# Down projection of three of four MLP quarters as seven block products per pair of weight tiles

## The chip, the cores and the metric

One core of a Trainium2 chip runs the whole kernel in one launch. The metric is the device time in microseconds (us) from start to end of an execution. Engines: TensorE (PE in the profile, its weight loads PEld), VectorE (DVE), ScalarE (ACT), GpSimd (POOL), SyncE (SP, which issues the transfers).

## The reference, cut to what matters

One layer of a hybrid decoder: 512 prompt tokens and 8 decode tokens, 1024 channels, three token mixers on one normalised input, merged by gates, then an MLP. The change is in the MLP's second matrix product:

```python
def merge_and_mlp(h, gates, y_a, y_b, y_c, w_out, norm_mlp_g, w_up, w_down):
    mixed = gates[0] * y_a + gates[1] * y_b + gates[2] * y_c
    h = h + mixed @ w_out
    hn = rmsnorm(h, norm_mlp_g)
    return h + jnp.square(jax.nn.relu(hn @ w_up)) @ w_down      # 1024 -> 4096 -> 1024
```

## The kernel before, in words

Activations lie transposed: 128 channels on the partitions, 520 tokens (512 + 8) along the free dimension, in two halves of `HALF` = 260. Each weight matrix is streamed in units of 128 output channels by 1024 input channels (`KC` = 8 blocks of 128x128, 512 KB). Every float32 operand is split in a high part (rounded to fp32r) and a low part (the rest), and a product is three matmuls of 260 columns: high x high, high x low, low x high. A tick is one unit with one half: 8 blocks x 3 = 24 matmuls into one PSUM bank. `TICKS` lists them in TensorE's order (`project`); VectorE's `take` reads the bank after each tick.

A unit goes through these hands: SyncE loads it (`load_unit`, L549) into one of `MR` = 8 raw slots of the MLP when the unit that had the slot has been split; ScalarE copies it to the high part (`split_hi`, L693 through `copy`) once the unit two before it has been used; GpSimd subtracts for the low part (`split_lo`, L668); TensorE waits for the low part.

The MLP goes by four quarters of the 4096 hidden channels. A quarter is 8 "up" units and 8 "down" units, 16 ticks each. In an up tick n (tile t = n // 2, half h = n % 2) VectorE's `take` makes `mt` (relu times the norm, L994), ScalarE's `hidden` squares it to `msq` (L930) and at once copies its high part to `hidh` (L693), and VectorE makes the low part of tick n-1 in `hid_split` (`hidl`, L991) after the take of tick n. A down tick adds its bank to the residual `hT` (L991). In the MLP six PSUM banks go round, so that TensorE can be up to six ticks ahead of VectorE's takes.

Each engine carries out its own instructions in the order of the program, which walks through the ticks: at tick k ScalarE first makes due high parts of weights (`SPLIT_AFTER`), then `hidden`; VectorE first `take`, then `hid_split`; GpSimd the due low parts. Semaphores make all other order: `made` (ticks done by TensorE), `dve_took`, `m_sq`, `hid_hi`, `hid_lo`, `w_hi`, `w_lo`. Beside this SyncE's queue carries 48 window copies of up to 2 MB.

Of the kernel before, what the change touches and what calls it, by code (L numbers as in the profile page):

```python
# [8 lines left out]
F32 = mybir.dt.float32  # L9
# [7 lines left out]
P = 128  # L17
# [25 lines left out]
def make_units():  # L43
# [30 lines left out]
    for q in range(QUARTERS):  # L74
        for t in range(KC):
            unit("up", KC * q + t, "w_up", KC * q + t, KC, [("up", 0, KC, "x", KC * q + t)])
        for t in range(KC):
            unit("down", KC * q + t, "w_down", KC * q + t, KC, [("down", 0, KC, "hidden", KC * q + t)])
    return out


QUARTERS = 4
QT = DFF // P // QUARTERS
UNITS = make_units()
# [3 lines left out]
TICKS = []  # L88
for _u, _unit in enumerate(UNITS[:U_END]):
    for _j, _job in enumerate(_unit["jobs"]):  # L90
        for _h in range(2):
            TICKS.append((_u, _job, _h, _j == len(_unit["jobs"]) - 1 and _h == 1))
# [9 lines left out]
def at(kind, tile, half=1):  # L102
    return AT[kind, tile, half]


# [15 lines left out]
_last = {}  # L121
FIRST, LEAD = 4, 4
for _k in range(NT):
    _ring = RING if _k < UP_TICK else RING + ["S0", "S1", "Z"]
    BANK.append({FIRST - 1: "S0", FIRST: "Z", FIRST + 1: "S1"}.get(_k, _ring[_k % len(_ring)]))
# [3 lines left out]
LO = []  # L129
_n = [0, 0]  # L130
for _u, _unit in enumerate(UNITS):
    _v = _u < 3 or _u == U_MLP + 1 or _u % 2 == 1 and _unit["kind"] in ("g0", "g1", "g2", "ab", "c", "out")
    _n[_v] += 1
    LO.append((_v, _n[_v]))
SPLIT_AFTER, LOAD_AT = {}, {}
for _u in range(3, NUNITS):
    SPLIT_AFTER.setdefault(LAST_TICK[_u - 2] if _u < U_END else END_TICK - 4 + _u - U_END, []).append(_u)
WR = 3
MR = 8
for _u in range(WR + 2, NUNITS):  # L140
    _ahead = WR if _u < U_MLP else MR
    LOAD_AT.setdefault(FIRST_TICK[_u - _ahead], []).append(_u)
LSTEPS = GH // 2 * 2 * QB
# [164 lines left out]
_n = 0  # L308
# [7 lines left out]
def decoder_step(nc, x, o):  # L316

    ctx = ExitStack()
    with ctx:
# [96 lines left out]
        mraw = place("mraw", [P, MR, KC, P], R)  # L416
        mlow = place("mlow", [P, MR, KC, P], R, F32R)
        mhigh = place("mhigh", [P, KC, KC, P], R + 21264, F32R)
        h2 = place("h2", [P, TOK], R + 9240)
        hacc = place("hacc", [P, TOK], R + 9760)  # L420
        rstdb = place("rstdb", [P, TOK], R + 10280)
        hvar = place("hvar", [P, 2, TOK], R + 10800)
        mt = place("mt", [P, 2, HALF], R + 11840)
        msq = place("msq", [P, 2, HALF], R + 12360)
        hidh = place("hidh", [P, QT, TOK], R + 12944, F32R)
# [41 lines left out]
        hsum_made, hvar_made, hln_made, hroot_made = (sem(n) for n in ("hsum_made", "hvar_made", "hln_made", "hroot_made"))  # L467
        m_sq, hid_hi, hid_lo = (sem(n) for n in ("m_sq", "hid_hi", "hid_lo"))
        ysq_made, yg_made, yacc_made, ysum_made, yvar_made, yln_made, yroot_made, y_made = (
# [3 lines left out]
        def raw(u):  # L473

            if u < U_MLP:
                return wraw[:, u % WR], w_in_slot[u % WR], 16 * (u // WR + 1)
            m = u - U_MLP
            return mraw[:, m % MR], m_in_slot[m % MR], 16 * (m // MR + 1)
# [6 lines left out]
        def low(u):  # L485
            if u == 2:
                return third[:, 1]
            return mlow[:, (u - U_MLP) % MR] if u >= U_END else wlo[:, u % 2]

        def half(h):  # L490
            return slice(h * HALF, (h + 1) * HALF)

        def took(k):
            return dve_took, k + 1
# [44 lines left out]
        def _(sp):  # L539
            def load_unit(u):  # L540
                unit = UNITS[u]
                if u >= U_MLP + MR:
# [108 lines left out]
        def _(pool):  # L651
# [14 lines left out]
            def split_lo(u):  # L666
                pool.wait_ge(w_hi, u + 1)
                nc.gpsimd.tensor_tensor(low(u), raw(u)[0], high(u).bitcast(F32), ALU.subtract).then_inc(w_lo, 1)  # L668

            def qd_zero(_):  # L670
                pool.wait_ge(xl_made, KC)
                nc.gpsimd.memset(qd[:], 0.0).then_inc(qd_zero_made, 1)

            stages = dict(qd_zero=qd_zero)
            for k, (u, job, h, last) in enumerate(TICKS):
                for v in SPLIT_AFTER.get(k, []):
                    if not LO[v][0]:
                        split_lo(v)
                for stage, n in PLAN[2 * k] + PLAN[2 * k + 1]:
                    if stage in stages:  # L680
                        stages[stage](n)

        @block.scalar
        def _(act):
# [263 lines left out]
            for k, (u, job, h, last) in enumerate(TICKS):  # L948
# [33 lines left out]
        def _(dve):  # L982
# [63 lines left out]

            plain = dict(sq=sqT, sk=skT, sv=svT, dq=dqT, dk=dkT, dv=dvT)

            def take(k):
                u, job, h, last = TICKS[k]  # L1050
                kind, tile = job[0], job[4]
                src = bank[BANK[k]][:, 0:HALF]
                root = rstd[:, half(h)]
                if kind in plain:
                    if kind == "dv" and tile == 0 and h == 0:
# [3 lines left out]
                    if kind in ("dq", "dk", "dv") and tile >= 2:  # L1059
                        n = HALF if h == 0 else S - HALF  # L1060
                        dst = by_residue(plain[kind][:, tile, 0:S])[:, h * HALF // 4:(h * HALF + n) // 4, :]
                        rows = [in_order(a[:, 0:n]) for a in (src, root)]
                        if h == 0:
                            tt(dst, *rows, ALU.mult).then_inc(dve_took, 1)
                        else:
                            link(tt(dst, *rows, ALU.mult))
                            tt(plain[kind][:, tile, S:TOK], src[:, n:HALF], root[:, n:HALF], ALU.mult).then_inc(dve_took, 1)
                    else:
                        tt(plain[kind][:, tile, half(h)], src, root, ALU.mult).then_inc(dve_took, 1)
                elif kind == "cc":  # L1070
# [72 lines left out]
                else:  # L1143
                    t = tile % KC
                    before = at("out", t, h) if tile < KC else at("down", tile - KC, h)
                    dve.wait_ge(dve_took, before + 1)
# [187 lines left out]
            for k, (u, job, h, last) in enumerate(TICKS):  # L1334
# [28 lines left out]
        def _(pe):  # L1363
# [24 lines left out]
            def x_total():  # L1388
                pe.wait_ge(consts_made, 4)
                pe.wait_ge(xacc_made, KC)  # L1390
                for h in range(2):
                    dst = open_bank(pe, "x_var", h)
                    mm(dst[:, 0:HALF], ones[:], xacc[:, half(h)], True, True).then_inc(of(written, "x_var", h), 1)

            def project(k, part):
                u, (kind, k0, nkc, what, tile), h, last = TICKS[k]
                act_h, act_l, a0 = source[what]
                if part == 0:
# [10 lines left out]
                for kc in range(part * nkc // 2, (part + 1) * nkc // 2):  # L1409
# [4 lines left out]
                    elif kind == "down" and tile % KC == 0:  # L1414
                        pe.wait_ge(hid_lo, 2 * tile + 2 * kc + h + 1)
                    wh, wl = high(u)[:, k0 + kc, :], low(u)[:, k0 + kc, :]
# [412 lines left out]
```

## Time and profile before

| | us |
|---|---|
| runs | 1039.56, 1039.63, 1040.22 (median 1039.63) |
| the profiled execution | 1039.1, its span 1037.3 |
| TensorE busy | 1017.4 (98%) |
| VectorE, ScalarE, GpSimd busy | 471.7, 404.5, 303.9 |
| granted TensorE clock, mean | 0.997 |

The profile is of one execution. The span runs from the first to the last instruction; 1.8 us of the time lie around it. Busy time of an engine counts its instructions as recorded; a VectorE instruction that has started but is held up inside counts as busy.

### The profile page before, as it was taken

What the parts mean: (1) busy time and instruction counts of PE and PEld (TensorE: products, weight loads), DVE (VectorE), ACT (ScalarE), POOL (GpSimd) and SP (SyncE); (2) the same over time, 40 slices, a digit from 0 to 9 for tenths busy, and PEclk for the clock granted to TensorE, in tenths of its full rate; (3) what the DMA queues carried; (4) which work ended last, traced back from release to release, by engine and by line L of the source; (5) the groups of instructions that cost most, each with busy time, mean ns of one, the idle gap of its engine ahead of it and who ended that gap; (6) DMA issues with size and microseconds to landing.
All of it is one profiled execution on the core that took longest, in us unless ns stands there. A gap on an engine that the chain in (4) does not pass through costs nothing.

```text
span 1037.3 us, 21462 instructions
## 1 busy us (share of the span) xinstructions
PE 1017.4 (98%) x8570; PEld 931.2 (90%) x8570; DVE 471.7 (45%) x814; ACT 404.5 (39%) x732; POOL 303.9 (29%) x138
## 2 busy tenths in 40 slices
PE   7999999999999999999999999999999999999996
PEld 7987878787878786899999999999999999999996
DVE  6215478789255554254444566622123112212444
ACT  6115556576244422252333333442244134214532
POOL 1323232232212121111112211243434343434720
PEclk9999999999999999999999999999999999999998
DMA  8588887785876477524223249284655747467202
GB/s 300 187 289 298 301 285 235 256 279 185 314 252 206 144 250 235 212 82 168 98 90 94 91 140 339 102 303 152 256 206 211 263 153 260 177 226 282 72 2 83
DMA packets 65669, 209.47 MB, mean 202 GB/s; under 512 B 7833, under 2 KB 10138, under 8 KB 63266
## 3 DMA queue, kind: packets, MB, share of 16 engines
q1 hardware_dynamic: 65282, 207.75, 57.8%
q8 instruction: 69, 1.13, 0.4%
q10 hardware_dynamic: 288, 0.35, 0.1%
q14 instruction: 30, 0.25, 0.1%
HBM read 200.59 MB, written 51.48 MB: 243 GB/s over the span
## 4 chain that ended last, share of the span: by engine, by line
PE 94%; DVE 3%; issue 1%; ACT 1%; DMA 1%; SPq 0%; DVEq 0%; ACTq 0%
PE G L1365 62%; PE S L1365 15%; PE Z L1365 13%; PE OU L1365 2%; PE TR L1368 2%; DMA xraw<-in_xt_dram 1%; DVE mtmp L994 0%; PE TR L1365 0%; DVE macc L991 0%; DVE convy L994 0%; DVE pw L1210 0%; ACT mixh L693 0%; DVE wlo L991 0%; ACT whi L693 0%; PE S L1368 0%
## 5 line engine op out<-in xcount | busy, mean ns | idle before, releaser
L1365 PE MATMUL G<-xh,whi 128*128 128x260 f32 x1288 | 373.9, 290 | 7.9 <-DVE xl L994 7.2
L1365 PE MATMUL G<-xl,whi 128*128 128x260 f32 x1288 | 365.1, 283 | 0.0
L1365 PE MATMUL G<-xh,wlo 128*128 128x260 f32 x1288 | 364.6, 283 | 0.0
L668 POOL TENSOR_TENSOR wlo<-wraw,whi 128x1024 fp32r<-128x1024 f32 x60 | 147.4, 2456 | 490.2 <-ACT whi L693 490.2
L1365 PEld LDWEIGHTS G<-xh,whi 128*128 128x128 f32 x1288 | 243.4, 189 | 51.9 <-issue 50.3
L1365 PEld LDWEIGHTS G<-xh,wlo 128*128 128x128 f32 x1288 | 243.6, 189 | 0.0
L1365 PEld LDWEIGHTS G<-xl,whi 128*128 128x128 f32 x1288 | 243.5, 189 | 0.0
L668 POOL TENSOR_TENSOR wlo<-mraw,whi 128x1024 fp32r<-128x1024 f32 x55 | 132.6, 2410 | 197.0 <-ACT whi L693 197.0
L693 ACT ACTIVATE whi<-wraw 128x1024 fp32r<-128x1024 f32 (+1 forms) x84 | 88.0, 1048 | 226.2 <-PE G L1365 208.5
L693 ACT ACTIVATE whi<-mraw 128x1024 fp32r<-128x1024 f32 x56 | 59.4, 1061 | 154.9 <-PE G L1365 52.1
L991 DVE TENSOR_TENSOR tg<-G,rstd 128x260 f32<-128x260 f32 x48 | 20.5, 427 | 85.8 <-PE G L1365 85.8
L1365 PE MATMUL G<-hidh,whi 128*128 128x260 f32 x192 | 54.3, 283 | 0.0
L1365 PE MATMUL G<-hidh,wlo 128*128 128x260 f32 x192 | 54.2, 282 | 0.0
L1365 PE MATMUL G<-hidl,whi 128*128 128x260 f32 x192 | 54.1, 282 | 0.0
L991 DVE TENSOR_TENSOR hT<-hT,G 128x260 f32<-128x260 f32 x47 | 19.9, 423 | 73.3 <-PE G L1365 73.3
L1365 PE MATMUL S<-xh,whi 128*128 128x260 f32 x176 | 49.8, 283 | 0.0
L1365 PE MATMUL S<-xl,whi 128*128 128x260 f32 x176 | 49.8, 283 | 0.0
L1365 PE MATMUL S<-xh,wlo 128*128 128x260 f32 x176 | 49.8, 283 | 0.0
L1365 PE MATMUL G<-binh,whi 128*128 128x260 f32 x160 | 45.6, 285 | 1.3 <-issue 1.3
L1210 DVE TENSOR_TENSOR_SCAN pw<-psp 128x512 f32<-128x512 f32 (+3 forms) x33 | 46.3, 1404 | 1.1
L930 ACT ACTIVATE msq<-mt 128x260 f32<-128x260 f32 x64 | 26.5, 414 | 51.7 <-DVE mt L994 51.6
L1365 PE MATMUL G<-binh,wlo 128*128 128x260 f32 x160 | 45.2, 283 | 0.0
(272 smaller groups left out, 2052.8 us busy)
## 6 DMA issues: line engine op xcount, KB each, us to landing
wraw<-in_w_in_dram SPq DMA_DIRECT2D x65, 512.0 KB, 5.8
kv<-in_kpool_dram SPq DMA_DIRECT2D x128, 256.0 KB, 3.8
kv<-in_vpool_dram SPq DMA_DIRECT2D x128, 256.0 KB, 3.4
mraw<-in_w_up_dram SPq DMA_DIRECT2D x32, 512.0 KB, 3.7
mraw<-in_w_down_dram SPq DMA_DIRECT2D x32, 512.0 KB, 3.5
out_win_k_kept_dram<-in_cache_win_k_dram SPq DMA_DIRECT2D x8, 2047.0 KB, 9.3
out_win_v_kept_dram<-in_cache_win_v_dram SPq DMA_DIRECT2D x8, 2047.0 KB, 11.0
wraw<-in_w_ab_dram SPq DMA_DIRECT2D x8, 512.0 KB, 3.3
```

The lines of the kernel that those rows point to most:

```text
L668: nc.gpsimd.tensor_tensor(low(u), raw(u)[0], high(u).bitcast(F32), ALU.subtract).then_inc(w_lo, 1)
L693: return nc.scalar.activation(out, in_, ACT.Copy, **kw)
L930: nc.scalar.activation(msq[:, h], mt[:, h], ACT.Square).then_inc(m_sq, 1)
L991: return nc.vector.tensor_tensor(out, a, b, op)
L1210: link(nc.vector.tensor_tensor_scan(w_[:, ::-1], l[:, ::-1], l[:, ::-1], carry, ALU.add, ALU.bypass))
L1365: return nc.tensor.matmul(out, lhsT, rhs, start=start, stop=stop, **kw)
L1368: return nc.tensor.transpose(out, in_, ident[0:rows, 0:rows])
```

## The change

Two down units (output tiles t, t+1) of a quarter are taken as a pair. Their product is cut in 2 x 2 blocks: output tile (even, odd), input channels (blocks 0 to 3, blocks 4 to 7) and token half (0, 1), and computed by Winograd's form of Strassen's scheme, with seven block products of 4 blocks x 3 = 12 matmuls where there were eight. That is done in quarters 0 to 2 (`SEVEN` = 3, 12 pairs); the last quarter stays as it was.

- Weights: VectorE makes four sums of 128x512 a pair (`block_sum`) and their four low parts (`sum_low`), ScalarE the high parts of seven blocks of 128x512 (`block_hi`), GpSimd the low parts of the three blocks that are no sums (`plain_low`). The old whole-unit splits of these units go.
- Hidden activations: for the half h = 1, tiles 0 to 3 get the combination T1 in place of the plain split; tiles 4 to 7 get T2, T3 and T4 beside the plain one. Each is a VectorE subtraction, a ScalarE high part and a VectorE low part of 128x260. `hidden` now copies the high part of tick n-1 after the square of tick n, and `msq` is double.
- Products 4, 5, 6 go on accumulating in the banks of products 0, 1, 3. `take_product` reads seven banks a pair, one into `eacc`, which in the third quarter is added to three parts of `hT`.
- `MR` goes from 8 to 6 raw slots; the last two units of the last quarter get places of their own. A slot of a paired unit is free when the pair's last product is made.
- For the first pair of a quarter the weights are prepared during the up ticks 7 to 13 of that quarter, for the others during the pair before.

```diff
+SEVEN = 3
+SUM_AT = (1, 2, 3, 5)
+PLAIN_AT = (0, 4, 6)
+def pair_ticks(g):
+    if g % (KC // 2):
+        return [at("prod", g - 1, j) for j in range(7)]
+    last = at("up", 2 * g + KC - 1)
+    return [last - 8 + j for j in range(7)]
+    for _i, _j in enumerate((0, 0, 2, 2)):
+        SUMS_AFTER.setdefault(_t[_j], []).append((_g, _i))
+    for _i, _j in enumerate((3, 4, 5, 6)):
+        LOWS_AFTER.setdefault(_t[_j], []).append((_g, _i))
+    for _n_, _j in enumerate((0, 1, 1, 3, 3, 4, 5)):
+        HIGHS_AFTER.setdefault(_t[_j], []).append((_g, _n_))
+    for _i, _j in enumerate((3, 4, 5)):
+        PLAIN_LOWS_AFTER.setdefault(_t[_j], []).append((_g, _i))
...
+    if _t // KC >= SEVEN or _h == 0:
+        _names = ("B",)
+    elif _c < KC // 2:
+        _names = ("T1",)
+    else:
+        _names = ("T2", "T3", "B", "T4")
...
-MR = 8
+MR = 6
+NHB = 8
+NSB = 6
...
+            def plain_low(g, i):
+                j = PLAIN_AT[i]
+                pool.wait_ge(b_hi, 7 * g + j + 1)
+                pool.wait_ge(s_made, 4 * g + (3, 4, 4)[i])
+                nc.gpsimd.tensor_tensor(block_low(g, j), block_raw(g, j), block_high(g, j).bitcast(F32),
+                                        ALU.subtract).then_inc(b_lo_pool, 1)
...
             for k, (u, job, h, last) in enumerate(TICKS):
+                for g, i in PLAIN_LOWS_AFTER.get(k, []):
+                    plain_low(g, i)
                 for v in SPLIT_AFTER.get(k, []):
...
             def hidden(k, t, h):
                 n = 2 * t + h
                 act.wait_ge(dve_took, k + 1)
-                if n >= 2:
-                    act.wait_ge(hid_lo, n - 1)
-                nc.scalar.activation(msq[:, h], mt[:, h], ACT.Square).then_inc(m_sq, 1)
+                if t >= 2:
+                    act.wait_ge(hid_lo, HID_AFTER[2 * t - 3])
+                nc.scalar.activation(full("B", t, h), mt[:, h], ACT.Square).then_inc(m_sq, 1)
+                if n % (2 * KC):
+                    hid_high(n - 1)
+                if n % (2 * KC) == 2 * KC - 1:
+                    hid_high(n)
+
+            def hid_high(n):
+                t, h = n // 2, n % 2
                 act.wait_ge(m_sq, n + 1)
-                copy(hidh[:, t % KC, half(h)], msq[:, h]).then_inc(hid_hi, 1)
+                for name in SPLITS[n]:
+                    if name != "B":
+                        act.wait_ge(t_made, SUM_N[name, t])
+                    copy(split_of(name, t, h)[0], full(name, t, h)).then_inc(hid_hi, 1)
...
                 if job[0] == "up":
                     hidden(k, tile, h)
+                for g, j in HIGHS_AFTER.get(k, []):
+                    block_hi(g, j)
...
             def hid_split(n):
                 t, h = n // 2, n % 2
-                dve.wait_ge(hid_hi, n + 1)
-                tt(hidl[:, t % KC, half(h)], msq[:, h], hidh[:, t % KC, half(h)].bitcast(F32),
-                   ALU.subtract).then_inc(hid_lo, 1)
+                dve.wait_ge(m_sq, n + 1)
+                for name in SPLITS[n]:
...
+                    tt(full(name, t, 1), a, b, ALU.subtract).then_inc(t_made, 1)
+                for name in SPLITS[n]:
+                    dve.wait_ge(hid_hi, HID_N[name, t, h])
+                    hi, lo = split_of(name, t, h)
+                    tt(lo, full(name, t, h), hi.bitcast(F32), ALU.subtract).then_inc(hid_lo, 1)
...
                 take(k)
+                for g, i in LOWS_AFTER.get(k, []):
+                    sum_low(g, i)
+                for g, i in SUMS_AFTER.get(k, []):
+                    block_sum(g, i)
...
+                name, c0_, h = (("B", 0, 0), ("T1", 0, 1), ("T2", 4, 1), ("T3", 4, 1), ("B", 4, 0), ("B", 4, 1),
+                                ("T4", 4, 1))[j]
...
+                    if g % (KC // 2) == 0:
+                        pe.wait_ge(hid_lo, HID_N[name, t, h])
+                    mm(out, wh, ah, kc == 0 and j < 4, False, skip_group_check=True)
+                    mm(out, wh, al, False, False, skip_group_check=True)
+                    ins = mm(out, wl, ah, False, kc == KC // 2 - 1, skip_group_check=True)
```

## Rows read from the trace of the kernel before

**Rows 1.** The page: busy time by engine, granted clock, chain that ended last.
```profile
PE 1017.4 (98%) x8570; PEld 931.2 (90%) x8570; DVE 471.7 (45%) x814; ACT 404.5 (39%) x732; POOL 303.9 (29%) x138
PEclk9999999999999999999999999999999999999998
PE 94%; DVE 3%; issue 1%; ACT 1%; DMA 1%; SPq 0%; DVEq 0%; ACTq 0%
```

**Rows 2.** Stretches: us, busy of PE, PEld, DVE, ACT, POOL, PEclk, DMA, GB/s.
```profile
656.90:702.70 45.80, 45.80 (x380) 45.68 (x379) 22.23 (x41) 22.52 (x44) 17.11 (x7) 1.00 0.57 205
702.70:748.80 46.10, 46.10 (x387) 46.10 (x386) 9.03 (x18) 9.21 (x10) 19.23 (x8) 1.00 0.59 213
748.80:794.90 46.10, 46.10 (x386) 46.10 (x385) 12.72 (x30) 20.37 (x38) 19.27 (x8) 1.00 0.59 212
```

**Rows 3.** Timeline of TensorE where quarter 0 goes from up to down.
```profile
702.58 0.28 PE L1365 MATMUL G<-xh,wlo 128*128 128x260 f32 x1
702.70 0.28 PE L1365 MATMUL G<-hidh,whi 128*128 128x260 f32 x1
```

**Rows 4.** Chain of waits that ended last, in order of time: start, us, what.
```profile
688.43 5.77 PE S L1365 x48
```

**Rows 5.** Groups by line and shape: count | busy, mean ns | idle before.
```profile
L668 POOL TENSOR_TENSOR wlo<-mraw,whi 128x1024 fp32r<-128x1024 f32 x55 | 132.6, 2410 | 197.0 <-ACT whi L693 197.0
L991 DVE TENSOR_TENSOR hidl<-msq,hidh 128x260 fp32r<-128x260 f32 x64 | 42.8, 670 | 4.4 <-ACT hidh L693 4.4
L991 DVE TENSOR_TENSOR wlo<-wraw,whi 128x512 fp32r<-128x512 f32 x2 | 1.4, 689 | 4.8 <-ACT whi L693 4.8
L811 ACT ACTIVATE psp<-pz 128x512 f32<-128x512 f32 x12 | 7.6, 632 | 0.4
```

**Rows 6.** Timeline of VectorE, ScalarE and GpSimd at the same place.
```profile
702.97 0.43 DVE L994 SCALAR_TENSOR_TENSOR mt<-G,rstdb 128x260 f32<-128x260 f32 x1 [1.95 <-PE G L1365]
703.31 0.42 DVE L991 TENSOR_TENSOR hidl<-msq,hidh 128x260 fp32r<-128x260 f32 x1
704.82 1.98 DVE L991 TENSOR_TENSOR hidl<-msq,hidh 128x260 fp32r<-128x260 f32 x1 [1.08 <-ACT hidh L693]
704.10 2.41 POOL L668 TENSOR_TENSOR wlo<-mraw,whi 128x1024 fp32r<-128x1024 f32 x1 [3.37 <-ACT whi L693]
702.96 1.06 ACT L693 ACTIVATE whi<-mraw 128x1024 fp32r<-128x1024 f32 x1 [1.53 <-PE G L1365]
703.92 0.41 ACT L930 ACTIVATE msq<-mt 128x260 f32<-128x260 f32 x1
704.36 0.42 ACT L693 ACTIVATE hidh<-msq 128x260 fp32r<-128x260 f32 x1
```

**Rows 7.** Timeline at the end of the last up stage.
```profile
971.76 10.10 POOL L668 TENSOR_TENSOR mlow<-mraw,mhigh 128x1024 fp32r<-128x1024 f32 x4
974.38 2.63 DVE L991 TENSOR_TENSOR hidl<-msq,hidh 128x260 fp32r<-128x260 f32 x1
977.27 2.30 DVE L991 TENSOR_TENSOR hidl<-msq,hidh 128x260 fp32r<-128x260 f32 x1
982.20 0.19 PEld L1365 LDWEIGHTS G<-hidh,mhigh 128*128 128x128 f32 x1 [0.15 <-DVE hidl L991]
```

**Rows 8.** Timeline: GpSimd beside VectorE in the attention part, and a take beside GpSimd.
```profile
207.31 0.55 DVE L994 SCALAR_TENSOR_TENSOR psp<-pz,psp 128x384 f32<-128x384 f32 x1
207.90 3.01 DVE L1210 TENSOR_TENSOR_SCAN pw<-psp 128x384 f32<-128x384 f32 x1
207.30 2.79 POOL L668 TENSOR_TENSOR wlo<-wraw,whi 128x1024 fp32r<-128x1024 f32 x1 [7.60 <-ACT whi L693]
711.62 0.42 DVE L991 TENSOR_TENSOR hT<-hT,S 128x260 f32<-128x260 f32 x1 [2.45 <-PE S L1365]
709.87 2.40 POOL L668 TENSOR_TENSOR wlo<-mraw,whi 128x1024 fp32r<-128x1024 f32 x1 [3.36 <-ACT whi L693]
```

**Rows 9.** Weight tiles of the MLP: issue to landing.
```profile
DMA to landing us min/median/max: 3.1/3.7/13.2
```

More of the change, by code:

```diff
@@ L89 @@
 for _u, _unit in enumerate(UNITS[:U_END]):
+    if _unit["kind"] == "sdown" and _unit["tile"] % 2 == 0:
+        for _j in range(7):
+            TICKS.append((_u, ("prod", 0, KC // 2, None, _unit["tile"] // 2), _j, _j == 6))
     for _j, _job in enumerate(_unit["jobs"]):
@@ L122 @@
 FIRST, LEAD = 4, 4
+_opened = UP_TICK
 for _k in range(NT):
     _ring = RING if _k < UP_TICK else RING + ["S0", "S1", "Z"]
-    BANK.append({FIRST - 1: "S0", FIRST: "Z", FIRST + 1: "S1"}.get(_k, _ring[_k % len(_ring)]))
+    _job = TICKS[_k][1]
+    if _job[0] == "prod" and TICKS[_k][2] >= 4:
+        BANK.append(BANK[at("prod", _job[4], {4: 0, 5: 1, 6: 3}[TICKS[_k][2]])])
+    elif _k >= UP_TICK:
+        BANK.append(_ring[_opened % len(_ring)])
+        _opened += 1
+    else:
+        BANK.append({FIRST - 1: "S0", FIRST: "Z", FIRST + 1: "S1"}.get(_k, _ring[_k % len(_ring)]))
     PREV.append(_last.get(BANK[-1]) if _k < UP_TICK or _last.get(BANK[-1], 0) > FIRST + 1 else None)
     _last[BANK[-1]] = _k
-LO = []
+LO, HI = [], []
 _n = [0, 0]
 for _u, _unit in enumerate(UNITS):
+    HI.append(sum(not seven(u) for u in range(_u + 1)))
+    if seven(_u):
+        LO.append(None)
+        continue
     _v = _u < 3 or _u == U_MLP + 1 or _u % 2 == 1 and _unit["kind"] in ("g0", "g1", "g2", "ab", "c", "out")
@@ L491, in half, with plain, block_raw, block_low @@
             return slice(h * HALF, (h + 1) * HALF)
+        def plain(g, n):
+            return U_PAIR[g] + (n == 2), slice(KC // 2 * (n > 0), KC // 2 * (n > 0) + KC // 2)
+        def block_raw(g, j):
+            if j in SUM_AT:
+                return bsum[:, (4 * g + SUM_AT.index(j)) % NSB]
+            u, rows = plain(g, PLAIN_AT.index(j))
+            return raw(u)[0][:, rows]
+        def block_low(g, j):
+            if j in SUM_AT:
+                return slow[:, (4 * g + SUM_AT.index(j)) % NSB]
+            u, rows = plain(g, PLAIN_AT.index(j))
+            return mlow[:, (u - U_MLP) % MR, rows]
+        def block_high(g, j):
+            return bhigh[:, (7 * g + j) % NHB]
+        def split_of(name, t, h):
+            c = t % KC
+            if name == "B" or name == "T1":
+                return hidh[:, c, half(h)], hidl[:, c, half(h)]
+            i = int(name[1]) - 2
+            return th[:, i, c - KC // 2], tl[:, i, c - KC // 2]
+        def full(name, t, h):
+            c = t % KC
+            if name == "B":
+                return b12[:, c] if t // KC < SEVEN and c < KC // 2 and h else msq[t % 2][:, h]
+            return t1[:, c] if name == "T1" else tn[:, int(name[1]) - 2, t % 2]
         def took(k):
@@ L541, in load_unit @@
                 unit = UNITS[u]
-                if u >= U_MLP + MR:
+                if u >= U_ASIDE:
+                    sp.wait_ge(made, at("prod", NPAIRS - 1, 6) + 1)
+                elif u >= U_MLP + MR and seven(u - MR):
+                    sp.wait_ge(made, at("prod", pair_of(u - MR), 6) + 1)
+                elif u >= U_MLP + MR:
                     sp.wait_ge(*split(u - MR))
@@ new lines, in block_sum @@
+            def block_sum(g, i):
+                even, odd = raw(U_PAIR[g]), raw(U_PAIR[g] + 1)
+                top, end = slice(0, KC // 2), slice(KC // 2, KC)
+                if i == 0:
+                    dve.wait_ge(*even[1:])
+                    dve.wait_ge(*odd[1:])
+                m = 4 * g + i - NSB
+                if m >= 0:
+                    dve.wait_ge(made, at("prod", m // 4, SUM_AT[m % 4]) + 1)
+                if i == 0:
+                    a, b, op = odd[0][:, top], odd[0][:, end], ALU.add
+                elif i == 1:
+                    dve.wait_ge(s_made, 4 * g + 1)
+                    a, b, op = block_raw(g, SUM_AT[0]), even[0][:, top], ALU.subtract
+                elif i == 2:
+                    a, b, op = even[0][:, top], odd[0][:, top], ALU.subtract
+                else:
+                    dve.wait_ge(s_made, 4 * g + 2)
+                    a, b, op = even[0][:, end], block_raw(g, SUM_AT[1]), ALU.subtract
+                tt(block_raw(g, SUM_AT[i]), a, b, op).then_inc(s_made, 1)
@@ L1144, in take @@
                     t = tile % KC
-                    before = at("out", t, h) if tile < KC else at("down", tile - KC, h)
-                    dve.wait_ge(dve_took, before + 1)
+                    dve.wait_ge(dve_took, at("prod", (tile - KC) // 2, 6) + 1)
                     dve.wait_ge(made, k + 1)
```

151 lines of the change are left out of this document (135 added, 16 removed).

## The prediction

> **What bounds the kernel now.** I read the page first: TensorE is busy 98% of the span at a granted clock of nine tenths or more in nearly every slice, and 94% of the chain that ended last is TensorE [rows 1]. Then the stretches by stage: in an up stage and in a down stage of the MLP TensorE has no gap, VectorE is busy 22 of 46 us in the up stage and 9 in the down stage, GpSimd 17 and 19, ScalarE 23 and 9 [rows 2]. So matmuls set the time, and the other engines have room, much in the down stages and less in the up stages. Last the timelines of VectorE and GpSimd, because the change gives both much more to do, and they show what the page does not: the two hold each other up (below).
>
> One matmul follows the last by 0.12 us [rows 3]; 48 of them take 5.77 us, so 0.120 us each [rows 4], and a tick of 24 takes 2.88.
>
> **What the change removes.** A pair of down units was 4 ticks x 24 = 96 matmuls, and becomes 7 x 12 = 84. Over 12 pairs 144 matmuls go, x 0.120 = 17.3 us. All of it is on the path, since TensorE is it. The Trainium skill's VectorE: DVE Perf Modes, section on the TRN2 errata, gives a matmul 6 cycles beyond its columns at 2.4 GHz; the removed ones would then be worth 16.0 us (an estimate, 144 x 266 / 2400), and the result 1.3 us later. The trace's spacing of 0.120 stands against its 0.111, and the sum goes by the trace.
>
> **What it adds, in a down stage.** Per pair (10.08 us of matmuls) VectorE gets 4 sums and 4 low parts of 128x512 at 0.69 us each [rows 5]; instructions that follow at once start 0.08 before the end of the one in front (702.97 with 0.43 long, the next at 703.31 [rows 6]), so 8 x 0.61 = 4.9, and 7 takes x 0.35 = 2.4: 7.3 us. ScalarE gets 7 x 0.63 = 4.4 [rows 5]. GpSimd gets three of 128x512; the trace has only 128x1024, 2.41 us [rows 5]. From below half, 1.2; from above 2.4. I take 1.25, near the half, since the length goes with the elements: 3.75 a pair. [...]
>
> The price is in how VectorE and GpSimd share. The low part `hidl`, which reads two SBUF tensors, takes 0.42 us alone, but 1.98 when it starts at 704.82 while GpSimd works from 704.10 to 706.51: it ends 0.29 after GpSimd [rows 6]. With four GpSimd instructions back to back (10.10 us for four) it gets in between two of them, and lasts 2.63 and 2.30 [rows 7]. The other way round GpSimd, started at 207.30 beside a VectorE instruction of 0.55, takes 2.79 in place of 2.41, and the scan behind it 3.01 [rows 8]. A take reads PSUM and one SBUF tensor and isn't held: 0.42 at 711.62 inside GpSimd's 709.87 to 712.27 [rows 8]. So the rule that I use: a VectorE instruction with two SBUF inputs and a GpSimd instruction exclude each other, whole instruction by whole instruction, in order of asking. In a pair that makes 4.9 + 3.75 = 8.6 us of exclusive work in 10.08, and takes can lie beside GpSimd's part. Walked through one pair in queue order VectorE falls 1.5 to 2 us behind and has caught up by the next pair. TensorE needs the take of product 3 before product 6, 2.5 us after its earliest end, and the low parts one to several us after they are made: no stall, 0 us, covered by that room. Without it the price would be the excess of VectorE (a rival below).
>
> **What it adds, in an up stage.** Here is the cost. Tiles 4 to 7 get 3 subtractions and 4 low parts for h = 1 instead of one low part, and ticks 7 to 13 also carry the first pair's 8 block instructions on VectorE, 7 on ScalarE and 3 on GpSimd, beside GpSimd's 2.41 a tile. I walk the queues with the durations above (260 wide: VectorE 0.42, spacing 0.35; ScalarE square and copy 0.41 and 0.42, `whi` 1.06 [rows 6]; hand-over between engines 0.05, and a take 0.27 after the next tick's first matmul [rows 3, 6]). Time 0 is the quarter's first matmul; tick n ends at 2.88(n+1).
>
> - Ticks 0 to 6: a tick costs VectorE take, wait for square and copy, low part; in odd ticks `whi` and then GpSimd's 2.41 come before. About 3.7 us in odd and 1.8 in even ticks, 5.5 for two against 5.76: level with TensorE.
> - Tick 7: take 23.3; the low part is held by GpSimd till 27.1; two block sums, the second behind the first: 28.4.
> - Tick 8: take (2.2 late), T1 and its low part: 30.1.
> - Tick 9: take 30.1. Now ScalarE has two block copies, then `whi` of tile 6 (30.7 to 31.8), then square and copy (32.5), and GpSimd's low part runs 31.8 to 34.2; VectorE stands until then, low part 34.5, two sums 35.7.
> - Tick 10: take 35.6 (3.7 late). GpSimd's first plain block 35.7 to 37.0 holds the three subtractions; the seven instructions end 39.3, a block's low part 40.0.
> - Tick 11: take 39.9. GpSimd's second plain block 40.0 to 41.2, behind it in its queue the low part of tile 7, whose `whi` came late too: 41.2 to 43.6. VectorE's low part 43.9, block 44.5.
> - Tick 12: take 44.4 (6.6 late), seven and a block: 47.9. Tick 13: take 47.8, held by the third plain block (47.9 to 49.2): 49.6, block 50.3. Tick 14: take 50.2, seven: 53.0. Tick 15: take 53.0, square, copy and low part of tick 14: 54.7, then three subtractions, and T2's low part of the last tile at 56.15, T4's at 57.2.
>
> TensorE's side: tile 7 should start at 40.3 but its low weights come at 43.6: 3.3 us of stall. It ends at 49.4; products 0 and 1 go till 52.3, and product 2 stands before its fourth block (53.4) until T2 of tile 7 is there, 56.2 (a released load starts 0.1 later or less [rows 7]): 2.8 us. Product 6 then waits about 0.25 for the take of product 3, behind four block sums. Together 6.4 us a quarter. The two stalls aren't independent: VectorE's chain to 56.15 binds, since from tick 9 on it is late against `made`; a tile 7 served sooner only moves the stall to product 2. In quarter 0 VectorE begins late already (the root of the norm) and I add 0.6. 3 x 6.4 + 0.6 = 19.8 us.
>
> **Other edits.** Fewer raw slots: a unit is asked for 10 us or more before its use, landing 3.7 us in the median, 13.2 at most [rows 9]: from 0 to, at the longest landing, some 3 us a quarter; I take 0. The last quarter keeps its form; its last low parts wait for GpSimd as before (0.15 us of TensorE [rows 7]): 0, either way under 0.5. The nine extra additions of the third quarter at 0.46 lie in pairs with room: 0. The banks of products 4 to 6 are those of 0, 1 and 3, covered by the same takes.
>
> **The sum.** -17.3 + 19.8 = +2.5 us on the profiled 1039.1: 1041.6. The median of the runs is 0.5 above it: 1042.1; I say 1042. Each quarter's chain of some 33 us from tick 7 has about thirty steps, and I hold it good to 1 us, which counts three times: 1039 to 1045 for this case.
>
> **Rivals.**
> - VectorE's chain is shorter and most of the gain is kept. For it: the exclusion is read off a few instances, and ScalarE and GpSimd could interleave better than I walk; in an up stage VectorE idles for over 23 us now [rows 2]. Against: the long waits at ticks 7, 9 and 11 are in the program's order. Half the stall: 3 x 3.2 less, 1032; no stall at all: 1022.
> - The pairs fall behind, in the steady down stage. If no take lies beside GpSimd, a pair is 4.9 + 2.4 + 3.75 = 11.1 us on VectorE against TensorE's 10.08: +1.0 each, 12 pairs, 1054. It decides from the point where VectorE's lateness passes the 2.5 us before product 6. Against: the walk catches up.
> - Weights land late with six slots: 3 us in each of three quarters at the longest landing, 1051. The median landing speaks against it.
>
> **Chances.** Walk right within its range 50%, shorter chain 27%, pairs behind 15%, late weights and other extra stalls 8%. About 0.2% (2.1 us) is what a measurement can tell. Of the 50% some 3 fall below 1037.5, 22 within 2.1 of 1039.63 and 25 above; the rivals are on their sides. Faster 0.29, same 0.23, slower 0.48. The range takes the half-stall case and most of the slower one: 1031 to 1051; the likeliest case's own is 1039 to 1045.
>
> **What would show it.** TensorE with 12 matmuls fewer a pair at the same 0.120; a gap of some 3 us before tile 7 of each of the first three up stages, released by GpSimd's `wlo`; another of some 3 us within the third product, released by VectorE's low part of T2; none in the pairs behind. `hidl` and its like with means far above 0.42. The prediction is wrong if these gaps are under 1 us or over 5, if gaps stand in later pairs, or if GpSimd's half-size instruction isn't near 1.25.

## The result, and the profile after

| | before | after | predicted |
|---|---|---|---|
| median of the runs, us | 1039.6 | 1048.57 (1047.31 to 1050.15) | 1042 (1031 to 1051) |
| ratio to before | 1 | 1.0083 [1.0069, 1.0096] | |
| profiled execution, its span | 1039.1, 1037.3 | 1050.15, 1048.4 | |
| TensorE busy, matmuls | 1017.4, 8570 | 1007.7, 8426 | 144 fewer |
| granted clock, mean | 0.997 | 0.992 | |

The kernel became 9.0 us slower; I had said 2.5. That is within the stated range of 1031 to 1051, but outside the 1039 to 1045 that I gave for my own walk. The profiled execution lies 1.6 us above its own median; 2.2 us of its surplus stands ahead of the MLP (first up matmul at 657.88, before at 655.66), in attention code that did not change and that varied between 656.5 and 659.6 over the kernels below. From there to the first matmul of the last down stage it is 332.37 us, before 323.88: +8.5, and that is what has to be explained.

The page after, beside [rows 1]: busy by engine, and the chain that ended last.

```profile
PE 1007.7 (96%) x8426; PEld 918.2 (88%) x8426; DVE 631.7 (60%) x1042; ACT 432.7 (41%) x828; POOL 306.7 (29%) x150
PE 76%; DVE 12%; issue 6%; ACT 4%; DMA 1%; SPq 1%; DVEq 0%; ACTq 0%
```

TensorE has less to do and is less of the chain (76%, before 94%), VectorE has 160 us more to do. Next, whom TensorE waited for in the MLP (us in total, times, longest):

```profile
PE G L1611 <- POOL wlo L812: 5.9, 2, 3.0
PE G L1611 <- DVE eacc L1166: 3.9, 1, 3.9
PE S L1611 <- POOL wlo L812: 2.9, 1, 2.9
PE G L1611 <- DVE tl L1166: 2.8, 2, 2.2
PE S L1611 <- DVE tl L1166: 2.2, 1, 2.2
```

Three waits of 3 us for GpSimd's `wlo` (tile 7 of an up stage), three for VectorE's `tl` (T2 in the third product), and one of 3.9 for `eacc`, which I had not. TensorE's timeline at these places:

```profile
702.30 0.39 PE L1611 MATMUL G<-xh,whi 128*128 128x260 f32 x1 [2.98 <-POOL wlo L812]
714.45 0.39 PE L1611 MATMUL S<-th,bhigh 128*128 128x260 f32 x1 [2.17 <-DVE tl L1166]
794.39 0.39 PE L1611 MATMUL G<-xh,whi 128*128 128x260 f32 x1 [2.95 <-POOL wlo L812]
806.54 0.59 PE L1611 MATMUL G<-th,bhigh 128*128 128x260 f32 x1 [2.17 <-DVE tl L1166]
887.63 0.39 PE L1611 MATMUL S<-xh,whi 128*128 128x260 f32 x1 [2.94 <-POOL wlo L812]
899.78 0.39 PE L1611 MATMUL G<-th,bhigh 128*128 128x260 f32 x1 [0.64 <-DVE tl L1166]
916.00 0.36 PE L1611 MATMUL G<-th,bhigh 128*128 128x260 f32 x1 [0.21 <-DVE hT L1166]
938.53 0.36 PE L1611 MATMUL G<-hidh,bhigh 128*128 128x260 f32 x1 [3.89 <-DVE eacc L1166]
```

Below I count a gap as the distance between two matmuls' starts less 0.12. Then these are 3.14, 2.33; 3.11, 2.34; 3.10, 0.80; 0.37 and 4.05 us. The stretches, columns as in [rows 2]: quarter 1 up and down, quarter 2 down, and two short ones behind a gap.

```profile
751.19:800.24 49.05, 46.10 (x386) 45.89 (x385) 31.50 (x52) 21.46 (x46) 18.98 (x9) 1.00 0.67 239
800.24:844.44 44.20, 42.02 (x338) 41.82 (x337) 39.39 (x69) 18.49 (x34) 20.16 (x11) 0.96 0.59 209
895.02:944.43 49.41, 43.99 (x338) 42.36 (x337) 43.62 (x75) 17.30 (x33) 20.37 (x11) 0.97 0.47 176
806.50:809.90 3.40, 3.36 (x16) 3.36 (x17) 3.29 (x9) 2.19 (x5) 0.00 (x0) 0.53 0.01 2
938.50:943.20 4.70, 4.67 (x26) 4.70 (x27) 1.31 (x4) 0.00 (x0) 0.00 (x0) 0.64 0.01 3
```

The up stage is 2.95 us longer than its 46.10 before. A down stage should be 336 x 0.120 = 40.3: quarter 1 took 44.2 and quarter 2 49.4. In the last two rows TensorE works without a break but at a granted clock near a half, the 1.2 GHz level: 13 matmuls behind the gap of 2.34 and 15 behind the one of 4.05 are 0.217 apart in place of 0.120. A third such stretch, 16 matmuls from 888.22, follows the gap before 887.63. Together 44 x 0.097 = 4.3 us.

Groups behind [rows 5] (count | busy, mean ns | idle before):

```profile
L1166 DVE TENSOR_TENSOR hidl<-msq,hidh 128x260 fp32r<-128x260 f32 x52 | 65.9, 1270 | 44.6 <-ACT hidh L846 44.6
L1166 DVE TENSOR_TENSOR slow<-bsum,bhigh 128x512 fp32r<-128x512 f32 x48 | 57.3, 1194 | 0.1
L812 POOL TENSOR_TENSOR wlo<-mraw,whi 128x1024 fp32r<-128x1024 f32 x31 | 76.9, 2485 | 116.1 <-ACT whi L846 116.1
L822 POOL TENSOR_TENSOR mlow<-mraw,bhigh 128x512 fp32r<-128x512 f32 x36 | 58.6, 1645 | 86.8 <-DVE bsum L1166 66.7
```

`hidl` takes 1.27 in the mean and `slow` 1.19 where they take 0.42 and 0.69 alone: 28 of all 64 `hidl` and 29 of the 48 `slow` last over 1 us, so being held is now common on VectorE. It is on GpSimd too: `mlow` has a mean of 1.65 and a shortest of 1.27, which bears out the estimate of 1.25.

### The profile page after: what moved, and what is told of

Same layout as the page of the kernel before. It is cut to its first block, busy times and chain, and to the rows that moved or that the text cites. A ratio compares the mean times of both kernels' runs of the same rounds, so it can differ in the third digit from the quotient of the medians.

```text
span 1048.4 us, 21764 instructions
## 1 busy us (share of the span) xinstructions
PE 1007.7 (96%) x8426; PEld 918.2 (88%) x8426; DVE 631.7 (60%) x1042; ACT 432.7 (41%) x828; POOL 306.7 (29%) x150
## 3 DMA queue, kind: packets, MB, share of 16 engines
HBM read 200.59 MB, written 51.48 MB: 240 GB/s over the span
## 4 chain that ended last, share of the span: by engine, by line
PE 76%; DVE 12%; issue 6%; ACT 4%; DMA 1%; SPq 1%; DVEq 0%; ACTq 0%
PE G L1611 52%; PE Z L1611 10%; PE S L1611 10%; PE OU L1611 2%; PE TR L1614 2%; DVE tn L1166 1%; DVE slow L1166 1%; DVE hT L1166 1%; DVE bsum L1166 1%; DVE mt L1169 1%; ACT whi L846 1%; DVE tl L1166 1%; DVE hidl L1166 1%; ACT hidh L846 1%; ACT msq L1083 1%
## 5 line engine op out<-in xcount | busy, mean ns | idle before, releaser
L812 POOL TENSOR_TENSOR wlo<-mraw,whi 128x1024 fp32r<-128x1024 f32 x31 | 76.9, 2485 | 116.1 <-ACT whi L846 116.1
L1166 DVE TENSOR_TENSOR hidl<-msq,hidh 128x260 fp32r<-128x260 f32 x52 | 65.9, 1270 | 44.6 <-ACT hidh L846 44.6
L822 POOL TENSOR_TENSOR mlow<-mraw,bhigh 128x512 fp32r<-128x512 f32 x36 | 58.6, 1645 | 86.8 <-DVE bsum L1166 66.7
L1083 ACT ACTIVATE msq<-mt 128x260 f32<-128x260 f32 x52 | 21.8, 418 | 124.8 <-DVE mt L1169 124.8
L1166 DVE TENSOR_TENSOR slow<-bsum,bhigh 128x512 fp32r<-128x512 f32 x48 | 57.3, 1194 | 0.1
L1611 PE MATMUL G<-binl,whi 128*128 128x260 f32 x160 | 45.3, 283 | 0.0
L846 ACT ACTIVATE bhigh<-bsum 128x512 fp32r<-128x512 f32 x48 | 29.9, 629 | 36.2 <-DVE bsum L1166 35.1
```

The costliest lines, as they stand in the source:

```text
L822: nc.gpsimd.tensor_tensor(block_low(g, j), block_raw(g, j), block_high(g, j).bitcast(F32), ALU.subtract).then_inc(b_lo_pool, 1)
L846: return nc.scalar.activation(out, in_, ACT.Copy, **kw)
L1083: nc.scalar.activation(full("B", t, h), mt[:, h], ACT.Square).then_inc(m_sq, 1)
L1166: return nc.vector.tensor_tensor(out, a, b, op)
L1611: return nc.tensor.matmul(out, lhsT, rhs, start=start, stop=stop, **kw)
```

## The experiments

Ratios are to the kernel before, from the same chip, with their 95% interval. The expectations were written before each run. They call the version with both repairs `e_both`, the best one `e_best`, the one with the additions one a tick `e_late`. Two theories were open. **A**: the third quarter's additions make its pairs longer on VectorE than on TensorE. **C**: the up stage's stalls come from the order in ScalarE's queue, in which `hidh` of an even tick stands one tick late behind block copies and `whi`; VectorE waits for it, GpSimd for `whi`. The rival to both (B against A, D against C): VectorE and GpSimd simply have too much exclusive work, and order does not matter.

### ScalarE copies an even tick's high part at once

```diff
-                if n % (2 * KC):
+                if n % 2 == 0 and n % (2 * KC):
                     hid_high(n - 1)
-                if n % (2 * KC) == 2 * KC - 1:
+                if n % 2 == 0 or n % (2 * KC) == 2 * KC - 1:
                     hid_high(n)
```

> The kernel after, with ScalarE copying the plain high part of an even tick right behind its square and not a tick later. Theory C (VectorE's chain in the up stage is long because it stands in odd ticks until ScalarE has made whi, square and copy, and then until GpSimd has ended): at tick 7 and 9 VectorE no longer stands 2 to 4 us each, and the gaps at tile 7 (9.35 us in all) and in the third product (5.5) go with two lower-clock stretches (3.2): about 1031. Rival D (the chain is bound by the exclusive work of VectorE and GpSimd, whatever the order): 3 us or less gained, 1045 or above.

Measured: 1039.66 us, 0.9993 [0.9983, 1.0002]: 9 us of the change's loss are gone. VectorE's timeline before tile 7 of quarter 1 (the quarter starts at 751.19 in the kernel after and at 746.53 in this one):

```profile
776.14 2.05 DVE L1166 TENSOR_TENSOR hidl<-msq,hidh 128x260 fp32r<-128x260 f32 x1 [1.34 <-ACT hidh L846]
783.50 2.04 DVE L1166 TENSOR_TENSOR hidl<-msq,hidh 128x260 fp32r<-128x260 f32 x1 [1.92 <-ACT hidh L846]
792.34 2.28 DVE L1166 TENSOR_TENSOR hidl<-msq,hidh 128x260 fp32r<-128x260 f32 x1 [1.18 <-ACT hidh L846]
```

That was the kernel after: in each odd tick VectorE stands 1.2 to 1.9 us for `hidh` and is then held by GpSimd for 2 more. In this one:

```profile
775.44 0.42 DVE L1169 SCALAR_TENSOR_TENSOR mt<-S,rstdb 128x260 f32<-128x260 f32 x1
775.78 0.42 DVE L1166 TENSOR_TENSOR hidl<-msq,hidh 128x260 fp32r<-128x260 f32 x1
784.14 0.41 DVE L1166 TENSOR_TENSOR hidl<-msq,hidh 128x260 fp32r<-128x260 f32 x1
```

At these places there is no wait and no hold. The gaps in the third product are gone, those before tile 7 fall to 2.12, 2.23 and 2.24. C holds, but I had expected about 1031: part of what is left before tile 7 is in GpSimd's own queue, where tile 7's low part stands behind a plain block's.

```profile
784.09 2.23 POOL L822 TENSOR_TENSOR mlow<-mraw,bhigh 128x512 fp32r<-128x512 f32 x1 [2.80 <-ACT bhigh L846]
786.27 2.53 POOL L812 TENSOR_TENSOR wlo<-mraw,whi 128x1024 fp32r<-128x1024 f32 x1
```

ScalarE had finished tile 7's `whi` at 784.96, so the low part could have ended at about 787.4, 1.4 us earlier (whether that would gain anything is tried below). The third quarter's gaps stayed (4.07 at its last pair), as A wants.

### The third quarter's additions, moved

In the kernel after, `take_product` does them at the seventh product. I moved the twelve to up ticks of the last quarter, first one a tick in ticks 2 to 13:

```diff
-                if q == SEVEN - 1 and j == 6:
-                    dve.wait_ge(dve_took, k + 1)
-                    for part in (hT[:, t, half(1)], hT[:, t + 1, half(0)], hT[:, t + 1, half(1)]):
-                        link(tt(part, part, eacc[:, t // 2], ALU.add))
...
```

> The kernel after, with the twelve additions of eacc to hT taken out of the third quarter's pairs and put into up ticks 2 to 13 of the last quarter, one a tick. Theory A (these additions push VectorE past a pair's 10.08 us, so that only the third quarter's pairs slip): the gaps within those pairs (6.1 us together, 3.9 in the largest) and the stretch of lower clock behind the largest (1.7 us) go, about 1041 against 1048.6 of the kernel after. Rival B (the pairs slip by the exclusion of VectorE and GpSimd alone): gaps stay, above 1046.

Measured: 1047.81, 1.0064 [1.0051, 1.0077], where about 1041 had been expected. The quarter's down stage fell from 49.4 to 41.6 us, so A holds; but most was given back at the end of the last up stage, where VectorE now was late:

```profile
989.48 0.59 PE L1615 MATMUL G<-hidh,mhigh 128*128 128x260 f32 x1 [4.96 <-DVE hidl L1166]
```

That gap and the 18 matmuls at the lower clock behind it cost 5.1 + 1.75. So two at a time in the ticks 0, 2, ... 10, where GpSimd has nothing new:

```diff
+                if job[0] == "up" and tile // KC == SEVEN and h == 0 and tile % KC < 6:
+                    late_add(2 * (tile % KC))
+                    late_add(2 * (tile % KC) + 1)
```

> The kernel after with only the additions moved, two at a time in up ticks 0, 2, ..., 10 of the last quarter. In e_late the third quarter's pairs lost their gaps (the quarter's down part took 41.6 us in place of 49.4), but VectorE came late into the last quarter's down part, 5.1 us of gap and 1.7 of lower clock. If that return was the ticks of the additions being the last before it, the time is about 1041; if additions in the last up stage cost their time wherever they are, 1046 or above.

Measured: 1040.87, 1.0011 [1.0002, 1.002], 7.7 us under the kernel after; in the third quarter no gap behind the third product is over 0.25. That is what the additions cost where they stood; the table at the end finds 7.3 of it (5.8 of gaps, 1.5 of lower clock).

### The form with seven products in two quarters only

```diff
-SEVEN = 3
+SEVEN = 2
...
```

The additions are then in quarter 1. Under A the loss goes with them; if it belonged to quarter 2 for another reason (late weights, the way into the last quarter), it would stay.

> The kernel after with seven products in two quarters only (SEVEN = 2), so that the additions of eacc fall in the second quarter. In the kernel after the second quarter took 93.25 us against 92.2 of before and the third 99.99. Theory A: the second quarter now takes about 100, the time is 1047 to 1048.5. Rival E (the third quarter is slow for its place, its transfers or its clock, not for the additions): its loss goes and the second stays at 93: about 1041 to 1042.

Measured: 1049.71, 1.0086 [1.0073, 1.0099], 1.2 us above the range given for A, but with its sign: quarter 1 took 100.0 us (93.25 in the kernel after), and its last pair shows the gap:

```profile
845.28 0.36 PE L1611 MATMUL S<-hidh,bhigh 128*128 128x260 f32 x1 [3.89 <-DVE eacc L1166]
```

Quarter 2, plain now, took 93.6. With two quarters 1.0086, with three 1.0083: the form bought nothing in the third.

### Both repairs, and the best version

> Both edits, the late additions and the early copies. If theories A and C hold, no gap of 1 us stays in the seven-product quarters and most of the 17.3 us of matmuls saved shows: about 1023 to 1026. With B and D: above 1043. If only one holds, the time is that of its own run.

Early copies with one addition a tick: 1034.06, 0.9942 [0.9929, 0.9954], 8 us above what was expected; gaps of 2.2 before tile 7 were left, and 2.22 with a lower clock behind it in the last quarter. From this came the version with early copies, additions two at a time, and GpSimd making a tile's low part ahead of the plain block's of the same tick:

```diff
-                for g, i in PLAIN_LOWS_AFTER.get(k, []):
-                    plain_low(g, i)
                 for v in SPLIT_AFTER.get(k, []):
...
+                for g, i in PLAIN_LOWS_AFTER.get(k, []):
+                    plain_low(g, i)
```

> Early copies as in e_both; the twelve late additions two at a time in up ticks 0, 2, ..., 10 of the last quarter, ahead of GpSimd's low parts of its end; and GpSimd makes a tile's low part ahead of a plain block's that falls in the same tick. In e_both 2.2 us stood at tile 7 of each of three quarters and 2.2 us in the last quarter with 1.5 of lower clock behind. If these are queue order (theory C carried on), the gaps at tile 7 fall to about 0.8 and the last one to 0.3: 1034 less 4.3 and 3.6, about 1026. If they are exclusion (theory D), what goes in one place comes back in product 2: above 1032.

Measured: **1029.83, 0.9902 [0.9887, 0.9917]**, faster than both kernels. TensorE's gaps in quarter 1 of it:

```profile
790.63 0.39 PE L1616 MATMUL G<-xh,whi 128*128 128x260 f32 x1 [0.70 <-POOL wlo L812]
801.68 0.39 PE L1616 MATMUL G<-th,bhigh 128*128 128x260 f32 x1 [1.10 <-DVE tl L1166]
```

0.86 and 1.26 a quarter, and no stretch at the lower clock: -17.3 + 3 x 2.1 = -11 by this count. From the first up matmul to the last down stage it is 313.5 us, 10.4 under the kernel before; by the medians it is 9.6.

The expected 1026 was missed by 3.8 us, because the gap came back in the third product, as D had it. In the version before this one tile 7 had a gap of 2.24 and the third product none, and VectorE made T2's low part (`tl`) at the same instant. First that version's rows, then the best one's:

```profile
789.63 0.39 PE L1615 MATMUL G<-xh,whi 128*128 128x260 f32 x1 [2.08 <-POOL wlo L812]
798.77 0.77 DVE L1166 TENSOR_TENSOR tl<-tn,th 128x260 fp32r<-128x260 f32 x2
801.20 0.76 DVE L1166 TENSOR_TENSOR tl<-tn,th 128x260 fp32r<-128x260 f32 x2
```

Quarter 1 starts at 747.29 and 749.68, so `tl` starts 51.48 and 51.52 us into it, and the quarter takes 88.77 and 88.82. The swap on GpSimd served tile 7 sooner and gained nothing. The 4 us between the two versions lie in the last quarter, where the additions two at a time took away the gap of 2.22 and the 16 slow matmuls behind it (1.55).

The last edit tried was to put two sum low parts of a quarter's first pair later (one to the next tick, one behind product 0), so that T2 comes sooner.

> e_best with two of VectorE's low parts of block sums for a quarter's first pair later: that of product 3 after up tick 14, that of product 5 after product 0. In e_best TensorE stood 1.25 us in the third product of each of three quarters for T2 of tile 7. If VectorE's chain ahead of it is what binds, it ends 0.6 us sooner and the gap is 0.6: 1.9 us less, about 1028. If the chain is bound elsewhere, no change, 1030; if product 5 then waits, slower.

Measured: 1031.12, 0.9917 [0.9903, 0.993], not to be told apart from the best version. The gap in the third product fell to 0.65, but gaps of 0.3 to 0.4 stood at the products behind. From the first up matmul to the last down stage it took the same time (313.6 us, before this edit 313.5), as if VectorE's whole work ahead of these products were the limit there, so that an order that serves one product sooner serves the next later.

### Plain blocks' low parts on VectorE

If GpSimd's share only held VectorE up, VectorE might as well do it.

> The kernel after with the low parts of the plain blocks made by VectorE (ticks 3, 5 and 6) and not by GpSimd. Per pair VectorE then has 11 instructions of 128x512 and 7 takes, 6.7 + 2.4 = 9.1 us of 10.08, and GpSimd none. If the exclusion (2.2 us on average beside 1.3 of GpSimd's own) is the dearer, first and second quarter lose nothing in their pairs and the up stage's gaps shrink by 1 to 2 us a quarter: 1043 to 1046. If VectorE's own time is the dearer, the third quarter (10.5 us a pair) slips as before and the up stage's chain is as long: 1048 to 1051.

Measured: 1051.4, 1.0108 [1.0092, 1.0123], some 3 us slower than the kernel after by the medians and 2.6 by the ratios, whose intervals just overlap. The gaps before tile 7 fell to 2.0, but the third products had 3.5, 2.0 and 2.0, and the last pairs of quarters 0 and 1, which had none, 0.96 each. So GpSimd pays for itself, by some 3 us if at all. The likely reason, not tested, is that takes, which read PSUM, lie beside its instructions.

### What holds VectorE up

Three VectorE instructions more behind each down take of the kernel before: in quarter 0 an addition with two SBUF inputs, in quarter 1 one with an SBUF and a PSUM input, in quarter 2 a copy with one SBUF input. The copies and sums go to a tile that nothing reads.

> The kernel before, with three extra VectorE instructions on scratch behind each take of a down tick, so that some fall beside GpSimd's 2.41 us: in quarter 0 additions with two SBUF inputs (128x520), in quarter 1 with one input in SBUF and one in PSUM (128x260), in quarter 2 copies of one SBUF input (128x520). The rule of the prediction: in quarter 0 one instruction in each odd tick lasts until GpSimd has ended, 1 to 2.5 us in place of 0.7; in quarter 1 all last 0.42 to 0.43. For the copies it said nothing: 0.4 to 0.7 each if they are not held. If the rule is wrong, GpSimd's instructions grow and VectorE's don't. The time stays within 0.5 us of before.

One execution, 1050.24 us (min/median/max ns, first and last start):

```profile
L991 DVE TENSOR_TENSOR h<-h,hacc x48: 686/700/2898, 708.5 to 764.4; 128x520 f32<-128x520 f32 x48
L991 DVE TENSOR_TENSOR h<-hacc,TR x48: 414/424/426, 810.4 to 853.7; 128x260 f32<-128x260 f32 x48
L1349 DVE COPY h<-hacc x41: 420/431/2522, 902.7 to 939.8; 128x520 f32<-128x520 f32 x41
```

The form with PSUM was never held (0.426 at most in 48, of which 23 lay beside a GpSimd instruction). With two SBUF inputs 8 of 48 were held, up to 2.9 us, and 8 of the plain copies too, up to 2.5 (the view lists 41 of the 48), which no row of before shows. The Trainium skill's SBUF — State Buffer, section "SBUF: two separate sides", says this: the port pair that VectorE and GpSimd share is an exclusive lock for a whole instruction, which VectorE needs for two SBUF inputs or for a copy in a two-port mode. The rows agree in all three forms. The 10.8 us that the probe cost were not expected: three additions a tick are more than VectorE can make in quarter 0, it came late into quarter 1, and TensorE stood 8 us for a `wlo` at 761.7.

### Gaps of a known length

Does a gap itself bring the lower clock, or what is special about these places? In the kernel before, TensorE was made to wait at ten ticks for a chain of two or four copies by ScalarE.

> The kernel before, with TensorE made to wait for a chain of two or four extra copies on ScalarE at ten ticks of the MLP: seven gaps of about 3.0 us and three of 1.6 us, 26 us together, nothing else changed. Theory F (a gap itself brings the lower clock of 1.2 GHz, as seen behind three of the seven gaps above 2 us in the kernel after): behind some three of the seven long ones 13 to 17 matmuls come at 0.217 us, 1.3 to 1.7 us lost each, so 1039.6 + 26 + 4 to 8 = 1070 to 1074. Rival G (the lower clock comes from the heavier load of VectorE and ScalarE): no such stretch, 1065 to 1066.

Measured: 1071.88, 1.0308 [1.0288, 1.0327]. The gaps are four of 2.85, three of 2.89 and three of 1.56 us, 24.7 together. Behind four of the seven long ones, and none of the short ones, matmuls come at 0.217. One such stretch, and a part of another gap, in which TensorE stands:

```profile
922.60:926.00 3.40, 3.40 (x18) 3.40 (x17) 0.00 (x0) 0.00 (x0) 0.00 (x0) 0.52 0.00 0
704.10:704.50 0.40, 0.00 (x0) 0.00 (x0) 0.00 (x0) 0.40 (x1) 0.00 (x0) 0.50 1.09 389
```

These stretches hold 11, 15, 15 and 26 matmuls, 6.5 us. So a gap is enough, whoever makes it. Where the fall lies differs. In the second row the granted clock is 0.50 while TensorE still stands (it resumes at 704.57), and so it is in the kernel after ahead of the matmul at 806.54:

```profile
806.30:806.50 0.20, 0.00 (x0) 0.00 (x0) 0.20 (x2) 0.20 (x1) 0.00 (x0) 0.50 0.00 0
```

There the second matmul comes 0.38 behind the first, and the next ones at 0.217. Such a fall within the gap stands ahead of 7 of the 24 stretches of ten kernels; in the other 17 TensorE resumed at full speed and the clock fell 0.3 to 1.5 us later, at work. Over these kernels (the kernel after and nine others with gaps of this kind) there is such a stretch: behind gaps of 0.6 to 1.6 us in none of 26, of 1.9 to 2.4 in 6 of 15, of 2.8 to 3.6 in 13 of 19, of 4.0 to 5.2 in 5 of 5. What picks the instances was not settled. The Trainium skill's TensorE: Matmul & The Clock Gate, Part 1, gives a matmul at the lower level the time of its columns at 1.2 GHz, 260 / 1.2 = 216.7 ns; the trace agrees, 0.217.

## Why the prediction was right, and where it failed

| term, us | predicted | measured |
|---|---|---|
| 144 matmuls | -17.3 | -17.3 |
| gap before tile 7 | 3 x 3.3 | 3.14 + 3.11 + 3.10 = 9.35 |
| gap in the third product | 3 x 2.8 | 2.33 + 2.34 + 2.35 = 7.0 |
| wait before product 6 | 3 x 0.25 | 0.17 + 0 + 0.24 = 0.4 |
| extra in quarter 0 | 0.6 | 0 |
| third quarter's other pairs | 0 | 5.8 |
| lower clock | none | 3.0 |
| sum | +2.5 | +8.3 (the stretch: +8.5) |

In the third product of quarter 2 the gap is 0.80, but the 16 slow matmuls ahead of it took 1.55 more. With all of them the place costs 2.35 as in the other two quarters: VectorE's T2 sets that instant (55.35 us into quarter 1, 55.34 into quarter 2), and TensorE may come to it slow for nothing. So this clock loss stands in the third row. The last but one has 1.26 + 1.46, and 0.26 for the matmul at 806.54, slow from its start. Product 6 of quarter 1 did not wait: TensorE came to it late by that stretch.

**The number.** 1048.6 lies in the stated range because that range took in most of a rival, the pairs that fall behind; the case that I held likeliest ended at 1045. That the total was in range is in part luck. By the prediction's own sign, gaps in later pairs, it was wrong in the third quarter.

**Right.** The removed term: 8426 matmuls, spacing 0.120. The exclusion rule, by the probe and by the walk that stands on it. In quarter 1, from its start at 751.19 (predicted, measured): the take of tick 7 at 23.3, 23.2; of tick 10 at 35.6, 35.5; of tick 11 at 39.9, 39.6; tile 7's low part ends at 43.6, 43.1; take 12 at 44.4, 44.0; take 15 at 53.0, 52.2; T2's low part of the last tile ends at 56.15, 55.3. After thirty steps the walk was 0.9 us late. Of that 0.4 is also in TensorE's arrival (tile 7 began at 43.2, not 43.6), and 0.5 is what the gap in the third product is under its 2.8. One instant as an example, tile 7's low part behind the second plain block, whose 1.29 had been put at 1.25:

```profile
790.75 1.29 POOL L822 TENSOR_TENSOR mlow<-mraw,bhigh 128x512 fp32r<-128x512 f32 x1 [2.86 <-ACT bhigh L846]
791.99 2.35 POOL L812 TENSOR_TENSOR wlo<-mraw,whi 128x1024 fp32r<-128x1024 f32 x1
```

Also right: the first two quarters' pairs behind the first had no gap, and six raw slots cost nothing that a wait shows (no wait of TensorE over 0.2 us in the MLP is for a DMA).

**Wrong, the first step.** "The nine extra additions of the third quarter at 0.46 lie in pairs with room: 0." They are twelve, three in each of four pairs, and there was no room. My own walk had VectorE 1.5 to 2 us behind inside a pair of 10.08, and I never walked one of the third quarter. Its VectorE from one pair to the next:

```profile
911.83 0.42 DVE L1166 TENSOR_TENSOR eacc<-eacc,S 128x260 f32<-128x260 f32 x1
915.77 1.44 DVE L1166 TENSOR_TENSOR slow<-bsum,bhigh 128x512 fp32r<-128x512 f32 x1
919.18 1.45 DVE L1166 TENSOR_TENSOR slow<-bsum,bhigh 128x512 fp32r<-128x512 f32 x1
921.00 1.36 DVE L1166 TENSOR_TENSOR hT<-hT,eacc 128x260 f32<-128x260 f32 x3
923.00 0.42 DVE L1166 TENSOR_TENSOR eacc<-eacc,G 128x260 f32<-128x260 f32 x1
```

A pair is 923.00 - 911.83 = 11.17 us with hardly an idle instant, of which the three additions are 1.36; without them 9.8, just inside 10.08. So the rival "the pairs fall behind", with its 11.1 us a pair, was true of one quarter in three, by the additions and not by takes that GpSimd holds. In the quarter's last pair the three meet GpSimd's low parts of the next up tiles, whole instruction against whole instruction:

```profile
932.17 5.15 DVE L1166 TENSOR_TENSOR hT<-hT,eacc 128x260 f32<-128x260 f32 x3
937.96 0.42 DVE L1166 TENSOR_TENSOR eacc<-eacc,G 128x260 f32<-128x260 f32 x1
931.21 5.36 POOL L812 TENSOR_TENSOR wlo<-mraw,whi 128x1024 fp32r<-128x1024 f32 x2
```

Three additions, 1.36 us elsewhere, last 5.15. Product 4 of the last pair goes on in the bank of product 0, whose take into `eacc` (at 937.96) stands behind them: 4.05 us. Moving the twelve gave back 7.7 us, the gaps and the clock behind the last.

**Wrong, the second step.** "Together 6.4 us a quarter" prices a gap at its length. A gap of 2 us or more can be followed by a stretch at 1.2 GHz worth 1.1 to 2.5 us (11 to 26 matmuls at 0.097 more each), here 3.0 on the path for two of them. The profile of before could not show it: it has no gap over 0.2 in the MLP. But it had no term of mine either, not even as a bound.

**Half right.** "A tile 7 served sooner only moves the stall to product 2." It did: with GpSimd's two instructions swapped tile 7's gap fell from 2.24 to 0.86, the third product's rose from none to 1.26, and quarter 1 took the same time (88.77, 88.82). VectorE's chain binds, as I said. Its length I had as a thing given: I took the order of ScalarE's queue as it was and charged the exclusion for the rest. The first experiment shows that `tl` can start 51.5 us into the quarter and not 54.9, and that 9 us came from one copy's place in that queue, which had VectorE asking for the port just after GpSimd had taken it.

## What to carry to other kernels

When work moves from the engine that is the bound to one that shares a port, walk the other engine's queue through each kind of period that exists, the odd last one above all: a pair at 97% of the period's room is fine, one at 111% costs its excess at once and more where the surplus meets a neighbour's long instructions. Before giving up such a change look for the instruction that waits for its input at the head of a queue while the port is free; here moving one ScalarE copy and twelve additions turned +9.0 us into -9.6, while swapping two GpSimd instructions moved a gap and gained nothing. Price a gap of TensorE of more than some 2 us with a stretch at half clock behind it.

## What the runs showed of the hardware

- VectorE and GpSimd back to back take turns: `slow` beside three `mlow` in a row lasted 1.45 each time in place of 0.69, and GpSimd's three 5.02 in place of 3 x 1.27. A held instruction counts as busy, so 60% busy can mean an engine without room.
- A VectorE copy of one SBUF tensor is held by GpSimd like an addition of two (2.52 in place of 0.43), an addition with a PSUM input never (0.426 at most).
- Behind a gap of TensorE the granted clock can fall to 1.2 GHz for 11 to 26 matmuls. In 17 of 24 cases it fell 0.3 to 1.5 us after TensorE had resumed at full speed, while it worked without a break; in 7 it was down before the gap had ended. At an equal gap of 2 to 3 us this happens in some instances and not in others; what decides stays open.
